# A hybrid attention, RWKV and MLP model in one kernel: GpSimd's work in whole tiles instead of slices

## The reference

```
h    = rms_norm(x);  proj = h @ w_in
o_a  = dilated window attention, 3 groups x 8 heads   (from proj)
o_r  = RWKV-7 state recurrence, 8 heads of 64         (from proj)
x    = x + rms_norm((sig(g1)*(o_a*silu(z_a))@w_up_attn + sig(g2)*(o_r*silu(z_r))@w_up_rwkv) @ w_out)
# second block, layer A: gated MLP
u, v, z = split(rms_norm(x) @ a_w_in);  y = gelu(u) * (W_s @ layer_norm(gelu(v)) + b) * silu(z)
x    = x + rms_norm(y @ a_w_out)
# layer B: sliding window attention, 16 query heads, 4 key/value heads, with sinks
k, v = rms_norm(x) @ w_k, rms_norm(x) @ w_v;   q, z = split(rms_norm(x) @ b_w_in)
x    = x + rms_norm((attention(q, k, v) * silu(z)) @ b_w_out)
```

## Time and profile before

| | us |
|---|---|
| three runs | 2842.01, 2836.62, 2834.11 |
| median | 2836.62 |
| profiled execution | 2842.01 |
| its span, first to last instruction | 2840.2 |

### The profile page before, as it was taken

One profiled execution on the slowest core, in us unless ns is written; L12 is line 12 of the kernel. 1 busy time (PEld: TensorE's weight loads), 2 busy tenths in 40 slices (PEclk: granted clock), 3 DMA queues, 4 the chain that ended last, 5 costly groups with the idle time before them and its releaser, 6 DMA issues.

```text
span 2840.2 us, 44277 instructions
## 1 busy us (share of the span) xinstructions
PE 2707.1 (95%) x17968; PEld 2176.6 (77%) x17968; DVE 1264.2 (45%) x2338; ACT 810.1 (29%) x1607; POOL 1040.2 (37%) x1318
## 2 busy tenths in 40 slices
PE   6999999997999999999898999999998998999999
PEld 5787777875867777686787888788887887777777
DVE  4225252435847466484531433533335003377743
ACT  3444444444113131220212211211113003255531
POOL 2223232232322231321455133344444456435442
PEclk9999999998999999999998899999999996999999
DMA  3111111111101010111331211111111121111122
GB/s 125 41 45 41 42 45 49 45 45 38 35 17 55 28 49 28 34 46 61 152 119 61 74 45 46 43 45 45 45 45 38 52 67 56 45 38 45 43 109 84
DMA packets 200907, 154.02 MB, mean 54 GB/s; under 512 B 5120, under 2 KB 183680, under 8 KB 200064
## 3 DMA queue, kind: packets, MB, share of 16 engines
q1 hardware_dynamic: 186256, 106.44, 12.6%
q10 hardware_dynamic: 14448, 44.74, 4.1%
HBM read 128.10 MB, written 23.07 MB: 53 GB/s over the span
## 4 chain that ended last, share of the span: by engine, by line
PE 79%; DVE 12%; ACT 6%; issue 1%; POOL 1%; DMA 1%; ACTq 0%; DVEq 0%; SPq 0%; POOLq 0%
PE gemm L527 21%; PE gemm L529 19%; PE gemm L528 19%; ACT prob L1942 3%; DVE neg_logits L1488 2%; DVE prob L1503 2%; PE scores L578 1%; PE scores L769 1%; PE weighted L829 1%; PE weighted L605 1%; PE probs_t L766 1%; PE probs_t L590 1%; PE scores L904 1%; PE scores L758 1%; DVE stats L1492 1%
## 5 line engine op out<-in xcount | busy, mean ns | idle before, releaser
L490 POOL CAST w_hi<-w_raw 128x512 fp32r<-128x512 f32 x360 | 249.1, 692 | 1686.8 <-PE gemm L529 1640.6
L527 PE MATMUL gemm<-h_hi,w_hi 128*128 128x512 f32 x1936 | 799.6, 413 | 9.7 <-ACT q_t L1702 7.6
L529 PE MATMUL gemm<-h_hi,w_lo 128*128 128x512 f32 x1936 | 761.9, 394 | 0.0
L528 PE MATMUL gemm<-h_lo,w_hi 128*128 128x512 f32 x1936 | 761.0, 393 | 0.0
L492 POOL TENSOR_TENSOR w_lo<-w_raw,w_hi 128x256 fp32r<-128x256 f32 x720 | 608.2, 845 | 56.9
L527 PEld LDWEIGHTS gemm<-h_hi,w_hi 128*128 128x128 f32 x1936 | 366.8, 189 | 102.8 <-issue 23.1
L529 PEld LDWEIGHTS gemm<-h_hi,w_lo 128*128 128x128 f32 x1936 | 366.8, 189 | 80.5
L528 PEld LDWEIGHTS gemm<-h_lo,w_hi 128*128 128x128 f32 x1936 | 367.6, 190 | 66.8 <-issue 1.9
L1382 DVE TENSOR_TENSOR scaled_product<-gemm,norm_rstd 128x512 f32<-128x512 f32 x116 | 80.2, 691 | 352.9 <-PE gemm L529 346.8
L527 PE MATMUL gemm<-xn_hi,w_hi 128*128 128x512 f32 x320 | 132.4, 414 | 7.2 <-POOL xn_lo L501 3.7
L1106 DVE CUSTOM_DVE_ANT_0 neg_logits<-scores,bias_tile 128x128 f32<-128x128 f32 (+1 forms) x192 | 67.6, 352 | 148.7 <-PE scores L578 142.9
(11 more groups left out here) (423 smaller groups left out, 4262.9 us busy)
## 6 DMA issues: line engine op xcount, KB each, us to landing
w_raw<-in_w_in SPq DMA_DIRECT2D x73, 512.0 KB, 3.9
w_raw<-in_a_w_in SPq DMA_DIRECT2D x48, 512.0 KB, 3.7
gates_scratch<-o_f ACTq DMA_DIRECT2D x32, 256.0 KB, 2.0
merge_gates<-gates_scratch ACTq DMA_DIRECT2D x4, 2048.0 KB, 15.1
w_raw<-in_a_w_out SPq DMA_DIRECT2D x16, 512.0 KB, 3.4
w_raw<-in_b_w_in SPq DMA_DIRECT2D x16, 512.0 KB, 3.7
x_rows<-in_x SPq DMA_DIRECT2D x8, 512.0 KB, 8.3
w_raw<-in_w_out SPq DMA_DIRECT2D x8, 512.0 KB, 3.4
```

The source lines that it names most:

```text
L490: Q(pool.tensor_copy(hi[:, ks, :], raw[:, s, ks, :]))
L527: pe.matmul(G[b][:], whi[:, s, k, :], hi(k, h), start=first, stop=False)
L528: pe.matmul(G[b][:], whi[:, s, k, :], lo(k, h), start=False, stop=False)
L529: m = pe.matmul(G[b][:], wlo[:, s, k, :], hi(k, h), start=False, stop=last)
```

## The change

The slices are removed: each POOL job is one instruction on the whole tile. For a unit of 8 x 128 columns that is one cast instead of two and one subtraction instead of four; a gain product, a low part or a sum of squares is one instruction instead of four. The arithmetic, the buffers, the order, the waits between engines and all other engines' programs stay.

```diff
-            def parts(n, size):
-                return [slice(i, min(i + size, n)) for i in range(0, n, size)]
...
-                    for ks in parts(KT, 2):
-                        Q(pool.tensor_tensor(raw[:, s, ks, :], raw[:, s, ks, :], g[:, ks].unsqueeze(2).to_broadcast([P, 2, P]), ALU.mult))
+                    Q(pool.tensor_tensor(raw[:, s], raw[:, s], g.unsqueeze(2).to_broadcast([P, KT, P]), ALU.mult))
...
-                for ks in parts(nk, 4):
-                    Q(pool.tensor_copy(hi[:, ks, :], raw[:, s, ks, :]))
-                for ks in parts(nk, 2):
-                    Q(pool.tensor_tensor(lo[:, ks, :], raw[:, s, ks, :], hi[:, ks, :].bitcast(F32), ALU.subtract), E("w_split") if ks.stop == nk else None)
+                Q(pool.tensor_copy(hi, raw[:, s, 0:nk, :]))
+                Q(pool.tensor_tensor(lo, raw[:, s, 0:nk, :], hi.bitcast(F32), ALU.subtract), E("w_split"))
...
-                    for ts in parts(T, 256):
-                        Q(pool.tensor_tensor(yslo[:, i, ts], ys[:, i, ts], yshi[i][:, ts].bitcast(F32), ALU.subtract), E("xn_low") if ts.stop == T else None)
+                    Q(pool.tensor_tensor(yslo[:, i, :], ys[:, i, :], yshi[i][:].bitcast(F32), ALU.subtract), E("xn_low"))
...
-                        for ts in parts(T, 256):
-                            Q(pool.tensor_tensor(xnlo[:, k, ts], y2[:, k, ts], xnhi[:, k, ts].bitcast(F32), ALU.subtract), E("xn_low") if ts.stop == T else None)
+                        Q(pool.tensor_tensor(xnlo[:, k, :], y2[:, k, :], xnhi[:, k, :].bitcast(F32), ALU.subtract), E("xn_low"))
...
-                    for ts in parts(T, 256):
-                        Q(pool.tensor_tensor(sq_buf[0][:, ts], sq_buf[0][:, ts], sq_buf[1][:, ts], ALU.add), E("sq_added") if ts.stop == T else None)
+                    Q(pool.tensor_tensor(sq_buf[0][:], sq_buf[0][:], sq_buf[1][:], ALU.add), E("sq_added"))
...
-                        for ts in parts(T - 1, 256):
-                            Q(pool.tensor_tensor(raw_of[i][:, 1 + ts.start:1 + ts.stop], raw_of[i][:, 1 + ts.start:1 + ts.stop], oF[:, 5 + p, ts], ALU.add), E("mixed_next") if ts.stop == T - 1 else None)
+                        Q(pool.tensor_tensor(raw_of[i][:, 1:T], raw_of[i][:, 1:T], oF[:, 5 + p, 0:T - 1], ALU.add), E("mixed_next"))
```

## The result

The changed kernel takes 2909.0 us in the median (2909.05, 2904.11, 2908.98) against 2835.4 for the kernel before in four runs beside it: the ratio is 1.0251, with a 95% interval of 1.0234 to 1.0268. Six further runs of it lie between 2901.89 and 2912.30. (One of 3736.79 us, at a granted clock of 0.669 instead of 0.97, was disturbed and is left out.) The forecast was 2862 us with a range of 2838 to 2884. The direction was right and the size was not: +2.5% instead of +0.9%. The profiled execution spans 2906.3 us, 66.1 more than the one before.

A forecast was written before the change was run, and what follows sets the result against it. The prediction took PE as 79% of the chain, DVE 12%, POOL 1%, with DVE on the path in the last attention layer. Last layer +16, RWKV +13, layer A to B -4 made +25 us on 2836.6: 2862 us, range 2838 to 2884.

The forecast's parts named there:

- rival (a): POOL gives its turn back within a long instruction, so DVE waits as now: 2833 us, chance 0.13.
- Rival (b): Last layer's loop: DVE's waits would not grow and saved fixed parts would shorten the kernel: 2828 us, chance 0.07.
- The last layer: Last attention layer, a DVE and ACT loop: longer POOL holds lengthen DVE's waits, +16 us, ends +8 and +28.
- at nothing: Stages whose chain is PE alone (first attention, MLP, both output products): PE's slack and POOL's idle time cover delays, 0 us.
- The step from A to B: Layer A to layer B, POOL on the path: PE's 3.7 us wait for it goes, -4 us, ends 0 and -9.
- the third of the RWKV sum: RWKV chunks: a 2.25 us hold sometimes delays L1309, about ten at 0.28 us, +2.8 us, between 0 and 14.
- a fall of the clock as a sign that it is wrong: Forecast is wrong if the clock falls in stages where PE now idles more; no size given.
- the preparations: RWKV preparation and inversion, four pairs: DVE held by whole-tile POOL instructions, +10.3 us.
- The first place: RWKV, L1227 and L1228 in pairs 1 to 3: cast and subtraction hold them, 1.6 us each, +4.9 us.
- the eight products: RWKV, L1250 to L1253: cast and subtraction delay them, +1.3 in three pairs, +0.2 in pair 0, 4.1 us.
- the start of the inversion in pair 0: RWKV pair 0: two DVE products beside four POOL slices lose 1.3 us more.
- Rival (c): PE locks DVE and POOL in phase; the long hold meets L1309 every chunk, L1492 every quad: 2886 us, chance 0.12.

The follow-up runs named there:

- Experiments 1 and 2: Changed kernel with POOL's slices back only in RWKV's units: 2854.6 us; or back only from the last attention layer's input product on: 2888.2 us.
- experiment 3: Changed kernel with only RWKV's shifted add back in slices of 256 columns: 2891.2 us, ratio to the kernel before 1.0205.
- Experiment 6: Changed kernel with only the subtraction back in slices of 256 columns, all other POOL jobs whole: 2856.0 us, ratio to the kernel before 1.0073.
- experiment 7: Kernel before, slices kept, with extra DVE memsets ahead of the decay in chunks 7 and 11 of pairs 1 and 2: 2863.0 us, ratio 1.0096.
- Experiment 4: Changed kernel with the state's decay in the RWKV chunks made by ACT instead of DVE: 2882.7 us, ratio to the kernel before 1.0181.
- xn_whole: Kernel before with only the low part of xn between layers A and B whole: 2829.3 us against 2830.2, ratio 1.0007.
- slices_128: Kernel before with slices of 128 columns (casts 256) and the low part between layers A and B whole: 2834.3 us, ratio 1.0011.
- mixed: Kernel before with slices of 128 columns (casts 256) only in the last attention layer's units, and xn's low part and ys whole: 2827.3 us, ratio 0.9973.
- sub_sliced: The same run as Experiment 6: changed kernel with only the subtraction back in slices of 256 columns, 2856.0 us.

## Why the prediction was right in direction and wrong in size

**Right.** POOL's instructions last as long as reckoned, they hold DVE until they end (longest 2.39, 1.90 and 2.42 us; forecast 2.4, 2.3, 2.4), and rival (a), that POOL gives its turn back within an instruction, fell at once with those maxima. The rule of the Trainium skill, page SBUF — State Buffer, section "Who interferes with whom", that the first engine keeps the shared pair for the whole instruction, agrees with the trace up to 2.42 us. Rival (b) fell too: waits grew in the last layer and in RWKV, where they cost, and also in the MLP, where they don't. The last layer is +19.3 for +16, and the last product at nothing; the MLP is +1.1 and the two other output products +1.6 and +2.0, where nothing was put. Experiments 1 and 2 show the two stages apart.

**The step from A to B, -5.8 for -4, is partly luck.** PE's wait for POOL, 3.7 us, is gone as forecast, but 1.6 us of wait for ACT's squares came in its place. The rest is the clock, which the prediction had named as a possible extra of up to 5 us and left out of the sum: the higher level came back about three tiles earlier (granted clock 0.69 over the stretch instead of 0.64), and PE is busy 44.6 us there instead of 48.4.

**The step that failed** is the third of the RWKV sum: "A 2.25 us hold falls on it with chance 2.25/3.75 and costs (2.25 - 0.8)^2/(2 x 3.75) = 0.28 us on average", ten of them 2.8 us, at most 14. It measured 26.4. It rests on a sentence further up, "DVE pays this once for each group of instructions that arrive together, since one that has waited a hold out finds the next ones free". Three things were wrong in it.

1. *One hold for each meeting.* L1309 is two instructions, and POOL's jobs stand in a row, subtraction then shifted add. Each DVE instruction can lose a turn, so the wait is 2.9 to 4.3 us instead of at most 2.25 (chunk 7 above; experiment 3 takes 16.6 us away by cutting the second job alone). The cover itself was right: in the short chunk 11 it is 3.52 - 2.68 = 0.84 us (forecast 0.8), in the long chunks 4 and 7 it is 1.53. "The longer chunks cover all of it" was wrong, because two holds are more than 1.53.
2. *A random phase.* All engines are driven by PE, and pairs 1 and 2 repeat to 0.01 us. The number of hits is not an expectation; it is a fact of the schedule, to be read by laying the new durations at POOL's start times. I had done that for the last layer, where the result was 33 - 17 = +16, and not for the chunks. Experiment 6 shows the other face of it: with the shifted add 0.8 us later, pairs 1 and 2 are clear. I made no run that only moves the phase, so that part rests on reading.
3. *A pause costs its length.* Behind a pause of 2.7 us PE runs at the lower level for a time, 1.5 to 2.7 us more in the changed kernel (with the chunk behind) and 1.56 and 3.7 (1.25 + 2.44) with the pauses of 3.7 us in experiment 7, without any long POOL instruction. The prediction had named a fall of the clock as a sign that it is wrong, and had no term for it: over the chunks of pairs 1 and 2 the granted clock is 0.96 and 0.95 instead of 1.00 and 0.98.

Experiment 4 closes this term: with the decay off DVE, 25.4 of the 66 us are gone and the chunks are back.

**Also too small: the preparations,** 18.3 us for 10.3, and by errors 1 and 3. The first place (L1227 and L1228 of before) is 8.2 us for 4.9, the eight products 5.3 for 4.1, and the start of the inversion in pair 0 is 4.7 for 1.3. DVE in pair 1 of the changed kernel:

```profile
881.46 3.01 DVE L1215 TENSOR_TENSOR_SCAN cum_decay<-chunk_reset,log_decay 128x1024 f32<-128x1024 f32 x1
884.51 3.24 DVE L1216 TENSOR_TENSOR log_decay<-cum_decay,log_decay 128x1024 f32<-128x1024 f32 x1
...
902.08 1.95 DVE L1239 SCALAR_TENSOR_TENSOR a_mats<-kk_t,log_decay 64x1024 f32<-64x1024 f32 x1
904.06 3.31 DVE L1240 TENSOR_TENSOR b_k<-kk_a,cum_decay 64x1024 f32<-64x1024 f32 x1
```

The waits of these instructions are as forecast (L1228 at 3.3 us; it is 3.24). Against the earlier trace rows, the scan and the addition take 6.25 us instead of 4.03, +2.2 where 2.3 - 0.5 = 1.8 was reckoned. But PE now pauses for them, 2.19 us, and behind that pause its score matmuls run at a lower clock in pair 1 and not in pair 2:

```profile
888.71 2.54 PE L650 MATMUL scores<-consts_sb,stats 128*64 128x128 f32 x32 [2.19 <-DVE stats L1221]
...
1074.55 1.97 PE L650 MATMUL scores<-consts_sb,stats 128*64 128x128 f32 x32 [2.19 <-DVE stats L1221]
```

By the first of the eight products pair 1 is 3.2 us late, where 1.6 was forecast, and pair 2 only 2.2; the 1.0 between them is the clock. The products add 1.4, where 1.3 was forecast. In pair 0 the inversion begins with two DVE instructions that follow each other directly, and they meet two POOL jobs that do:

```profile
754.70 3.29 DVE L1264 TENSOR_TENSOR a_level<-a_ab,consts_sb 128x1024 f32<-128x1024 f32 x1
758.02 3.25 DVE L1268 TENSOR_TENSOR inv_t<-a_level,consts_sb 128x1024 f32<-128x1024 f32 x1
```

```profile
754.51 2.40 POOL L484 TENSOR_TENSOR w_lo<-w_raw,w_hi 128x1024 fp32r<-128x1024 f32 x1
757.34 2.85 POOL L501 TENSOR_TENSOR r_t<-r_t,o_f 128x1023 f32<-128x1023 f32 x1 [0.43 <-ACT o_f L1648]
```

L1264 takes 1.23 us at this place before the change, and L1268 1.65.

**Left out: the end of the first attention,** costed at nothing because PE was its chain. Its last 20 us are mostly a chain of DVE, where instructions are held too (L1118 on 34x512, which is L1130 of before and took 0.98 us at this place, takes 2.77 at 668.34 us): +3.7 of the +5.0. A stage that is PE's by its share need not be PE's at its end.

**Rival (c)** had the right kind, a fixed phase, and was still short with 2886, since it priced a hit with one hold and no clock. With the measured terms the sum is 26.4 + 18.3 + 19.3 - 5.8 + 5.0 + 3 = +66 where the forecast had 2.8 + 10.3 + 16 - 4 = +25.

**Open.** The 5.6 us that xn_whole gains in its stretch do not show in 11 runs. The stretch hangs on where PE's clock comes back: it takes 61.2 or 61.3 us at a granted clock of 0.64 in the three profiles that keep slices of 256 there, and with the same whole job 51.9 (slices_128), 55.7 (xn_whole), 56.9 (mixed) and 57.4 us (sub_sliced), at 0.66 to 0.74; slices of 512 give 51.7. The two profiles of the kernel before agree in it, which speaks against a stretch that varies from one execution to the next, but they are of executions of 2842.0 and 2835.6 us, and the median of the 27 runs beside xn_whole is 2830.2: no profile shows one of those. The mixed kernel's gain of 6.5 us is about that of its last layer alone (6.0), which again leaves nothing for the stretch. Open too is why the clock falls behind one pause of 2.19 us and not behind another.

## What to carry to other kernels

A long GpSimd instruction is priced by what it holds up, not by its own engine's time: look in the stage whose chain runs through DVE, and count each DVE instruction that follows another directly, as long as POOL has a job waiting too, since each can lose a turn. Keep slices short there (128 columns gained 6 us in the last layer), but not where another engine waits for POOL's whole job (slices_128, chunk 5). Where PE alone was the chain the size mattered by up to 3 us a stage. Where one engine drives all others, lay the new durations at the old start times instead of averaging over phases, and give a pause of PE a second term for its clock; in the chunks of this kernel it was 0 behind pauses of up to 1.5 us and 1.3 to 3.7 us behind longer ones.

## What the runs showed of the hardware

- Between two DVE instructions 0.03 us apart a waiting POOL instruction gets its turn and keeps it for 2.34 us; the second DVE instruction, 0.25 us of work, waits it out (4.81 us for the two).
- The longest wait grows in proportion to the columns of POOL's instruction: the longest L1492 is 0.51 us with slices of 128 columns, 0.79 with 256, 1.33 with 512 and 2.39 with 1024, which is 0.28, 0.56, 1.10 and 2.16 above its 0.23.
- In the chunks PE paused 1.0 to 1.5 us with no fall of the granted clock. Behind pauses of 1.68 (pair 0), 2.19 (slices_128), 2.7 and 3.7 us its matmuls started every 0.43 us instead of 0.23, for some 3 us in most of them, whether DVE's wait for POOL, memsets on DVE or ACT had caused the pause. Behind the pause of 2.19 us in the preparations the clock fell in pairs 1 and 3 and not in pair 2, so the length of the pause alone does not tell.
- A memset of 128x1024 on DVE takes 0.91 us and starts 1.19 us after the one before it when each waits for the last, 0.28 of it gap.
